# State-space projections in a new order, with two of five convolution taps on GpSimd

## The reference, cut to what matters

```python
zxbcdt = u @ w_in                                   # u: (256, 1024), w_in: (1024, 5184)
z   = zxbcdt[..., :2048]
xbc = silu(dwconv_centred(zxbcdt[..., 2048:5120], conv_w, conv_b))   # 5 taps, 3072 channels
dt  = softplus(zxbcdt[..., 5120:] + dt_bias)        # 64 step rows: 2 directions x 32 heads
x, B, C = xbc[:2048], xbc[2048:2560], xbc[2560:]    # B and C: 4 groups of 128 states
# context: only its final states are wanted:  sum over tokens of B^T (x * dt * decay), per group, both directions
# sequence: y = (C B^T * decay mask) (x dt) + C state * exp(cumulated decay), both directions, + d_skip x
# out = rmsnorm_by_group(y * silu(z)) @ w_out
```

## Time and profile before

| | us |
|---|---|
| median of three runs (lowest, highest) | 3063.94 (3062.34, 3069.13) |
| the profiled execution | 3061.89 |
| its span | 3060.1 |
| TensorE busy | 2890.5 |
| VectorE busy | 2267.7 |
| ScalarE busy | 1404.9 |
| GpSimd busy | 398.1 |

### The profile page before, as it was taken

One profiled execution on the slowest core, in us unless ns is written; L12 is line 12 of the kernel. 1 busy time (PEld: TensorE's weight loads), 2 busy tenths in 40 slices (PEclk: granted clock), 3 DMA queues, 4 the chain that ended last, 5 costly groups with the idle time before them and its releaser, 6 DMA issues.

```text
span 3060.1 us, 61776 instructions
## 1 busy us (share of the span) xinstructions
PE 2890.5 (94%) x24756; PEld 2772.1 (91%) x24756; DVE 2267.7 (74%) x3614; ACT 1404.9 (46%) x2279; POOL 398.1 (13%) x430
## 2 busy tenths in 40 slices
PE   5999999999999999999999999699989899999898
PEld 5999887899999988779999999599978899999898
DVE  7999565578878775556787888589867688777654
ACT  3446533444444563444444445544677344444342
POOL 0025001010200210200102012001026201102002
PEclk9999999999999999999999999799989899999899
DMA  9995302459968641125787885189522388676353
GB/s 342 350 373 158 124 9 97 131 191 326 335 232 283 214 152 64 54 72 186 255 319 263 312 324 170 58 309 327 186 82 72 132 302 322 235 261 212 111 186 131
DMA packets 172725, 632.19 MB, mean 207 GB/s; under 512 B 19169, under 2 KB 19553, under 8 KB 172001
## 3 DMA queue, kind: packets, MB, share of 16 engines
q1 hardware_dynamic: 123696, 450.79, 42.0%
q10 hardware_dynamic: 48816, 178.41, 16.9%
HBM read 628.07 MB, written 1.05 MB: 206 GB/s over the span
## 4 chain that ended last, share of the span: by engine, by line
PE 84%; DVE 11%; ACT 3%; issue 1%; DMA 1%; POOL 0%; DVEq 0%; ACTq 0%; POOLq 0%
PE psum L581 23%; PE psum L583 23%; PE psum L582 23%; DVE w_lo L549 3%; DVE xl L2151 2%; PE psum L599 1%; DVE ada_w L628 1%; PE psum L600 1%; DVE bc L2151 1%; PE psum L605 1%; PE psum L2299 1%; PE psum L1495 1%; PE psum L1498 1%; PE psum L2328 1%; PE psum L2219 1%
## 5 line engine op out<-in xcount | busy, mean ns | idle before, releaser
L581 PE MATMUL psum<-h_hi,w_hi 128*128 128x256 f32 x4464 | 1257.4, 282 | 1.2 <-ACT qn L1940 0.9
L582 PE MATMUL psum<-h_hi,w_lo 128*128 128x256 f32 x4464 | 1250.6, 280 | 0.0
L583 PE MATMUL psum<-h_lo,w_hi 128*128 128x256 f32 x4464 | 1249.0, 280 | 0.0
L549 DVE TENSOR_TENSOR w_lo<-raw,w_hi 128x1024 fp32r<-128x1024 f32 x852 | 1065.7, 1253 | 193.0 <-ACT w_hi L536 192.0
L536 ACT ACTIVATE w_hi<-raw 128x1024 fp32r<-128x1024 f32 x852 | 875.1, 1055 | 386.8 <-DMA raw<-stream_dram 229.4
L581 PEld LDWEIGHTS psum<-h_hi,w_hi 128*128 128x128 f32 x4464 | 843.1, 189 | 8.4 <-issue 5.3
L582 PEld LDWEIGHTS psum<-h_hi,w_lo 128*128 128x128 f32 x4464 | 843.3, 189 | 0.5
L583 PEld LDWEIGHTS psum<-h_lo,w_hi 128*128 128x128 f32 x4464 | 843.0, 189 | 0.0
L581 PE MATMUL psum<-u_hi,w_hi 128*128 128x256 f32 x1584 | 442.8, 280 | 0.0
L582 PE MATMUL psum<-u_hi,w_lo 128*128 128x256 f32 x1584 | 442.1, 279 | 0.0
L583 PE MATMUL psum<-u_lo,w_hi 128*128 128x256 f32 x1584 | 442.0, 279 | 0.0
(11 more groups left out here) (385 smaller groups left out, 3411.0 us busy)
## 6 DMA issues: line engine op xcount, KB each, us to landing
raw<-stream_dram SPq DMA_DIRECT2D x852, 512.0 KB, 4.2
ada_w<-ada_dram ACTq DMA_DIRECT2D x328, 512.0 KB, 4.7
tmp<-c_dram ACTq DMA_DIRECT2D x8, 512.0 KB, 3.7
x<-x_dram SPq DMA_DIRECT2D x1, 1024.0 KB, 9.9
ctx_x<-ctx_dram ACTq DMA_DIRECT2D x1, 1024.0 KB, 4.8
means<-means_dram ACTq DMA_DIRECT2D x1, 1024.0 KB, 4.8
out_dram<-tmp SPq DMA_DIRECT2D x1, 1024.0 KB, 3.9
const<-const_dram SPq DMA_DIRECT2D x1, 753.0 KB, 13.2
```

What stands on the lines that cost most here:

```text
L549: p.nc.vector.tensor_tensor(p.w_lo[:, slot].rearrange("p k m -> p (k m)"), p.raw[:, slot], p.w_hi[:, slot].rearrange("p k m -> p (k m)").b ...
L581: mm(out, p.w_hi[:, slot, k], hi, start=start, stop=False, skip_group_check=skip)
L582: mm(out, p.w_lo[:, slot, k], hi, start=False, stop=False, skip_group_check=skip)
L583: return mm(out, p.w_hi[:, slot, k], lo, start=False, stop=stop, skip_group_check=skip)
```

## The change

The units of the projections come as B, C, step rows, x (context: B, step rows, x). The separate state stage is gone. Between the units TensorE now turns finished pairs, makes the columns, B by C and, for the context, the states group by group (two behind units 15 and 19, two at the end); ScalarE copies them between its own steps and applies silu two tiles late instead of one. The step rows are computed right behind the first x tile. Weighted x (xw) is made per group and direction, 14 of the 16 instructions on GpSimd, two on VectorE. For the sequence GpSimd takes the middle tap with the bias (ScalarE's before) and tap 0 (VectorE's before), as two tensor_scalar and an add; VectorE keeps three taps. Z units 0 and 1 run between the last turned pairs, z unit t of the rest at step 2t-1 of the mixing loop (2t+1 before), and VectorE makes a gate behind the output in the same step, not before it. Some semaphores are shared under new names.

```diff
     dt = np.concatenate([w_in[:, 5120:5184], np.zeros((D, P - 64), np.float32)], 1)
-    return [by_tile(np.concatenate([xbc, dt], 1))]
+    xs, bc = xbc[:, : N_X * P], xbc[:, N_X * P :]
+    return [by_tile(np.concatenate([bc, dt, xs], 1))]
 
...
-        self.sconv_in = self.over("sconv_in", 32768, [P, 4, 264])
+        self.sconv_ctx = self.over("sconv_ctx", 32768, [P, 4, 264])
+        self.sconv_x = self.over("sconv_x", 65536, [P, 4, 264])
...
-        self.xw = self.over("xw", 0, [P, 2, 2048])
+        self.xw = self.over("xw", 65536, [P, 2, 2, 512])
+        self.tap = self.over("tap", 73728, [P, T])[:]
...
+SSD_BANKS = (5, 4, 7, 6)
+
+
+def turned_at(st, u):
+
+    if st.on_ctx and u in (6, 8):
+        return (u - 6) // 2
+    i = u - st.n_dt - 5
+    return 2 * st.on_ctx + i // 2 if i >= 0 and i % 2 == 0 and i // 2 < 6 else None
+
+
+def turned_pair(st, j):
+
+    if st.on_ctx:
+        return (N_X + 2 * j, N_X + 2 * j + 1) if j < 2 else (2 * j - 4, 2 * j - 3)
+    return 2 * j, 2 * j + 1
+
+
+def conv_tile(st, k):
+    return N_X + k if k < st.n_dt else k - st.n_dt
...
+    def turn(j):
+        s0, s1 = turned_pair(st, j)
+        pe.wait_ge(p.sem["act_done"], a("act_done") + (s1 - N_X + 1 if s1 >= N_X else s1 + n_bc + 1))
+        if j >= 2:
+            pe.wait_ge(p.sem["sturn_out"], a("sturn_out") + j - 1)
...
+        ins.then_inc(p.sem["sturned"], 1)
...
+    def columns_of(rows):
+        pe.wait_ge(p.sem["dt_ready"], a("dt_ready") + 1)
...
+        ins.then_inc(p.sem["cols_done"], 1)
+
+    def b_by_c(g):
+        pe.wait_ge(p.sem["act_done"], a("act_done") + N_BC + g + 1)
+        if g == 1:
+            pe.wait_ge(p.sem["cols_ready"], a("cols_ready") + 1)
+        if g >= 2:
+            pe.wait_ge(p.sem["cb_out"], a("cb_out") + g - 1)
...
+        ins.then_inc(p.sem["cb_done"], 1)
+
+    def state(g):
+        for d in range(2):
+            pe.wait_ge(p.sem["xw_ready"], a("xw_ready") + 2 * (2 * g + d) + 2)
+            if g:
+                pe.wait_ge(p.sem["state_out"], a("state_out") + 2 * g + d - 1)
...
+            ins.then_inc(p.sem["state_sum"], 1)
...
+    for u in range(2, st.n_conv + 1):
+        if u >= 4:
+            pe.wait_ge(p.sem["proj_out"], a("proj_out") + u - 3)
+        pe.wait_ge(p.sem["lo_ready"], u0 + u + 1)
         for k in range(UNIT):
...
+        if turned_at(st, u) is not None:
+            turn(turned_at(st, u))
+        if u == n_bc + 5:
+            columns_of(p.rows if st.on_ctx else p.soft)
+        if not st.on_ctx and u >= 12 and u % 2 == 0 and u < 20:
+            b_by_c((u - 12) // 2)
+        if st.on_ctx and u in (15, 19):
+            state((u - 15) // 4)
+    if st.on_ctx:
+        turn(last - 1)
+        turn(last)
+        state(2)
+        state(3)
+        pe.wait_ge(p.sem["state_out"], a("state_out") + 8)
     else:
-        for c in range(8):
-            one(1, c)
-    for c in range(st.n_conv % 8 + 1):
-        one(st.n_conv // 8, c)
+        pe.wait_ge(p.sem["proj_out"], a("proj_out") + st.n_conv - 1)
+        z_unit(p, pe, st.mix, 0)
+        turn(last - 1)
+        z_unit(p, pe, st.mix, 1)
+        turn(last)
 
 
 def ssd_in_scalar(p, act, st):
...
+    for u in range(st.n_conv + 1):
+        k = u if u < n_bc else u - 1
+        if u > 1:
+            split_hi(p, act, u0 + AHEAD + u)
+        act.wait_ge(p.sem["unit_done"], u0 + u + 1)
+        raw = p.psum[:, SSD_BANKS[u % 4], 0:T]
+        if u == n_bc:
+            f(p.rows[0:ROWS], raw[0:ROWS], ACT.Copy).then_inc(p.sem["proj_out"], 1)
+        else:
+            if k >= 4:
+                act.wait_ge(p.sem["conv_done"], a("conv_done") + k - 3)
+            t = conv_tile(st, k)
+            if st.on_ctx:
+                f(p.sxbc(t), raw, ACT.Identity, scale=w[:, t, 2:3], bias=bias[:, t : t + 1])
+            f(raw_in[:, k % 4, 2 : 2 + T], raw, ACT.Copy).then_inc(p.sem["proj_out"], 1)
+            if k >= 2:
+                silu(k - 2)
+        if u == n_bc + 1:
+            gate_steps(p, act, st)
+        if turned_at(st, u - 1) is not None:
+            turned(turned_at(st, u - 1))
+        if not st.on_ctx and u == n_bc + 3:
+            act.wait_ge(p.sem["dt_step"], a("dt_step") + 7)
+            f(p.row_parts[0:ROWS], p.rows[0:ROWS], ACT.Copy).then_inc(p.sem["gate_fn"], 1)
+        if not st.on_ctx and u > 12 and u % 2 and u < 21:
+            b_by_c((u - 13) // 2)
+        if st.on_ctx and u in (16, 20):
+            state((u - 16) // 4)
+    silu(st.n_conv - 2)
+    silu(st.n_conv - 1)
+    if turned_at(st, st.n_conv) is not None:
+        turned(turned_at(st, st.n_conv))
+    for j in range(2):
+        turned(6 + 2 * st.on_ctx + j)
+    if st.on_ctx:
+        state(2)
+        state(3)
...
 def ssd_in_gpsimd(p, pool, st):
...
+        norm_gpsimd(p, pool, st.next_norm)
+        pool.wait_ge(p.sem["cols_ready"], a("cols_ready") + 1)
+        for i in range(7):
+            weighted_x(p, pool, p.nc.gpsimd, st, i // 2, i % 2)
+        return
+    w = st.par(p, "conv").rearrange("p (t j) -> p t j", j=5)
+    bias, v = st.par(p, "conv_b"), p.nc.gpsimd
+    pool.wait_ge(p.sem["conv_pad"], a("conv_pad") + 8)
+    for k in range(st.n_conv):
+        u, t, src = k if k < st.n_dt else k + 1, conv_tile(st, k), raw_in[:, k % 4]
+        pool.wait_ge(p.sem["proj_out"], a("proj_out") + u + 1)
+        v.tensor_scalar(p.sxbc(t), src[:, 2 : 2 + T], w[:, t, 2:3], bias[:, t : t + 1], ALU.mult, ALU.add).then_inc(
+            p.sem["tap_step"], 1)
+        if k:
+            pool.wait_ge(p.sem["tap_done"], a("tap_done") + k)
+        v.tensor_scalar(p.tap, src[:, 0:T], w[:, t, 0:1], None, ALU.mult).then_inc(p.sem["tap_step"], 1)
+        pool.wait_ge(p.sem["tap_step"], a("tap_step") + 2 * k + 2)
+        v.tensor_tensor(p.sxbc(t), p.sxbc(t), p.tap, ALU.add).then_inc(p.sem["tap_done"], 1)
+
+
+def weighted_x(p, eng, engine, st, g, d):
+
+    a = st.at
+    eng.wait_ge(p.sem["sturn_out"], a("sturn_out") + 2 * g + 4)
+    if g:
+        eng.wait_ge(p.sem["state_sum"], a("state_sum") + 2 * g + d - 1)
+    heads, part = slice(d * SH + 8 * g, d * SH + 8 * g + 8), slice(g * 512, g * 512 + 512)
+    for c in range(2):
+        engine.tensor_tensor(
+            p.xw[:, d, c].rearrange("p (h n) -> p h n", h=8), p.x_tok[:, c, part].rearrange("p (h n) -> p h n", h=8),
+            p.scols[:, 0, c, heads].unsqueeze(2).broadcast_to([P, 8, 64]), ALU.mult,
+        ).then_inc(p.sem["xw_ready"], 1)
 
 
 def ssd_in_vector(p, dve, st):
-    a, u0, v = st.at, st.unit0, p.nc.vector
+    a, u0, v, n_bc = st.at, st.unit0, p.nc.vector, st.n_dt
     w = st.par(p, "conv").rearrange("p (t j) -> p t j", j=5)
-    dve.wait_ge(p.sem["conv_pad"], a("conv_pad") + 4)
-    for t in range(st.n_conv):
-        if t > 1:
-            split_lo(p, dve, u0 + AHEAD + t)
-        dve.wait_ge(p.sem["proj_out"], a("proj_out") + t + 1)
-        out, src = p.sxbc(t), p.sconv_in[:, t % 4]
-        for i, j in enumerate((0, 1, 3, 4)):
+    raw_in = p.sconv_of(st)
+    dve.wait_ge(p.sem["conv_pad"], a("conv_pad") + 8)
+    for k in range(st.n_conv):
+        u = k if k < n_bc else k + 1
+        if k == n_bc:
+            split_lo(p, dve, u0 + AHEAD + n_bc)
+        if u > 1:
+            split_lo(p, dve, u0 + AHEAD + u)
+        if st.on_ctx:
+            dve.wait_ge(p.sem["proj_out"], a("proj_out") + u + 1)
+        else:
+            dve.wait_ge(p.sem["tap_done"], a("tap_done") + k + 1)
+        t = conv_tile(st, k)
+        out, src, taps = p.sxbc(t), raw_in[:, k % 4], (0, 1, 3, 4) if st.on_ctx else (1, 3, 4)
+        for i, j in enumerate(taps):
             if i:
-                dve.wait_ge(p.sem["conv_step"], a("conv_step") + 3 * t + i)
+                dve.wait_ge(p.sem["conv_step"], a("conv_step") + (len(taps) - 1) * k + i)
             v.scalar_tensor_tensor(out, src[:, j : j + T], w[:, t, j : j + 1], out, ALU.mult, ALU.add).then_inc(
-                p.sem["conv_step" if i < 3 else "conv_done"], 1)
-    split_lo(p, dve, u0 + AHEAD + st.n_conv)
-    step = a("dt_step")
+                p.sem["conv_step" if i < len(taps) - 1 else "conv_done"], 1)
+        if k == n_bc:
+            step_rows(p, dve, st)
+        if k == n_bc + 3 and not st.on_ctx:
+            dve.wait_ge(p.sem["gate_fn"], a("gate_fn") + 6)
+            v.tensor_tensor(
+                p.row_parts[ROWS : 2 * ROWS], p.rows[0:ROWS], p.row_parts[0:ROWS].bitcast(F32), ALU.subtract
+            ).then_inc(p.sem["dt_ready"], 1)
+        if k == n_bc + 5:
+            dve.wait_ge(p.sem["cols_done"], a("cols_done") + 1)
+            v.tensor_copy(p.scols[:, 0].rearrange("p c r -> p (c r)"), p.psum[:, 3, 0 : 2 * ROWS]).then_inc(
+                p.sem["cols_ready"], 1)
+    if st.on_ctx:
+        dve.wait_ge(p.sem["cols_ready"], a("cols_ready") + 1)
+        dve.wait_ge(p.sem["xw_ready"], a("xw_ready") + 14)
+        weighted_x(p, dve, v, st, 3, 1)
...
         v.tensor_tensor(p.soft[0:ROWS], p.sin[0:ROWS], rows, ALU.subtract).then_inc(p.sem["dt_ready"], 1)
-
-
-
...
```

(38 more changed lines are left out.)

254 lines of the change are left out of this document (94 added, 160 removed).

## The result

The change makes the kernel slower: 3098.58 us (median of 5 runs, 3089.29 to 3103.80) beside 3069.13 for the kernel before on the same chip (5 runs, 3062.34 to 3073.48). The ratio is 1.0096, 95% interval 1.0077 to 1.0115, so +29.5 us. The forecast was 3077, that is +13 against its own reference of 3063.9; the sign is right, the size less than half of what came, and 3098.58 is above the range of 3060 to 3090.

What follows compares the result with a forecast made beforehand. TensorE, busy 94% of 3060.1 us, was taken as the bound. Context -17.7, sequence's projections +5.5 and mixing loop +24.9 gave +12.7, 3074.6 profiled, forecast 3077 at the median's offset; range 3060 to 3090.

Steps and rivals of the forecast that it cites:

- Part 1: Context projections up to the next norm's sum: 17.7 us saved, bounds -20 to -5.
- The price put on weighted x: Context: each 128x512 weighted x instruction on GpSimd taken at 1.25 us, between 0.9 and 3.4.
- Part 2: Sequence's projections up to the first exponential: 5.5 us longer, between -8 and +13.
- The columns' wait: Sequence's projections: TensorE stands 7.5 us behind unit 14, as VectorE copies the columns only after convolution 13.
- the one at turn 0: Sequence's projections: TensorE waits 5 us for silu 9 at turn 0, while the step rows hold ScalarE and GpSimd.
- that makes 2.9 us a tile: Sequence's convolutions: GpSimd's three new instructions, 0.53, 1.15 and 1.15 us, sum to 2.9 a tile, 3.5 at the upper end.
- rival 2: GpSimd bounds the sequence's convolutions at 3.5 to 3.8 us a tile, adding 6 to 10: 3085; chance 0.15.
- the tap saved is given back by the slower neighbours: Sequence's convolutions: VectorE's three taps and a split beside GpSimd take 3.14 us a tile, no less than four taps alone.
- Part 3: Mixing loop, first exponential to last products: 24.9 us longer than 112.2; +16.5 or +27 with other waits.
- The ring: Mixing loop's two z banks: z unit t needs the gate of t-2, so units 4 to 15 each wait 2.3 us.
- rival 1: The two z banks do not bind; the mixing loop is 2.7 us shorter: 3049; chance 0.12.
- A pair of steps takes 5.27 + 4.14: Mixing loop: 5.27 us until the z unit starts plus 4.14 for it and products, 9.4 instead of 7.07.

Runs made afterwards that it cites:

- e7_ctx_only: Kernel before with only the change's context part; sequence projections, turns and mixing loop stay old: 3046.96 us, ratio 0.9935 to the kernel before.
- e1_ring: Changed kernel with z units 2 to 15 put back from step 2t-1 to 2t+1: 3051.92 us, ratio 0.9967 to the kernel before.
- e2_gate_first: Changed kernel, z units still early, VectorE making the gate before the output: 3068.07 us, ratio 1.0013 to the kernel before.

## Why the prediction was right or wrong

**Part 1 was right.** Forecast -17.7 for the profiled execution, measured -16.3 in it and -17.8 in e7_ctx_only. The price put on weighted x, 1.25 us from no row, stands between what four took beside VectorE (5.52, 5.20, 4.81 us) and alone (2.04 for two):

```profile
1906.49 5.52 POOL L2286 TENSOR_TENSOR xw<-x_tok,scols 128x512 f32<-128x512 f32 x4 [31.93 <-ACT x_tok L2179]
...
1947.66 2.04 POOL L2286 TENSOR_TENSOR xw<-x_tok,scols 128x512 f32<-128x512 f32 x2 [5.37 <-PE psum L2127]
...
1907.46 4.82 DVE L2312 SCALAR_TENSOR_TENSOR xl<-sconv_ctx,par,xl 128x256 f32<-128x256 f32 x4
```

The third row is the disturbance: four taps of VectorE take 4.82 us beside it instead of 2.04, three times, 8 us in all where "some 5" were allowed. The step rows' wait was 4.4 where 5.8 follows from the forecast. Of the 6.7 at the turns of x, 5.5 is the wait ahead of the last turn, for which the forecast's tail has 0.9 + 2.0 + 0.8 = 3.7: the third disturbance falls on just these taps. The 1.2 at the turn ahead of it are near the 1.4 that the forecast gave to silu 5.

**Part 2 had the waits at the right places and GpSimd's part wrong.** The columns' wait (7.5 forecast, measured 7.2) and the one at turn 0 (5, measured 4.8) are there. They are only in part the order's own: with the early copy the first is 3.8, without GpSimd's taps they are 4.8 and 2.5, and with both edits 0.4 and 2.4. No run has GpSimd at the 2.9 us that the forecast worked with, so that its two waits came out nearly as measured, while GpSimd took more, is in part luck. The step that failed is "that makes 2.9 us a tile": 0.53, 1.15 and 1.15 became 0.79, 1.08 and 1.47, a tile each 3.40. That is rival 2's mechanism in part only: GpSimd is slower than VectorE and keeps it waiting, but it is not the bound of the stretch, since behind the columns TensorE's own work is. Of the 6 to 10 that rival 2 put on the forecast 3.2 came, though against four taps on VectorE the two taps cost 8.1. A second step failed with it: "the tap saved is given back by the slower neighbours". VectorE's taps and split went from 3.10 to 2.8 a tile, and it then waited for GpSimd. From 243 to 270 us VectorE was indeed slowed by its neighbour; in the sequence's projections the neighbour hardly slowed it, it kept it waiting. A slip in the same sum: from 244.33 to 268.48 there are 22 starts and so 21 gaps, 1.15 us each and not 1.10, and 1.21 without the two short ones; with it a tile is still under 3.0 and nothing in the forecast changes.

The rule of the Trainium skill, GPSIMD Engine Reference, Key points, on instructions of two SBUF inputs, agrees here: VectorE's four taps took 4.82 beside weighted x, and GpSimd's add took 1.47 beside VectorE's split, which reads two, where it had taken 0.74 beside none. The one-input rate of the same page's Engine selection, against which the forecast argued, would give 0.5 for the product, as an estimate; it took 1.08.

**Part 3 had the right mechanism, and its sum lacked a term.** The ring binds, at units 4 to 15, twelve times, for a gate that stands behind the output: rival 1 falls, e1_ring and e2_gate_first show it. The wait was put at 2.3 and is 1.81 (the z unit starts 4.9 us after the even rows, not 5.2, and would be there after 3.1, not 2.93). The step that failed is "A pair of steps takes 5.27 + 4.14 (z unit and products, ...) = 9.4" (5.23 by its own terms, 0.5 us in all): the 4.14 behind the wait were taken at the full clock, though the same text, in part 2, charged clock for pauses by the 0.77 of the earlier trace rows. A pair takes 10.67. In the terms of the sum: waits 21.8 us instead of 27.6, lower clock 14 to 17 instead of 0, less the 2.7 of the two units that left the loop. With that term the upper bound of part 3 would have been some 42 (an estimate, 27 and 14 to 17) and the range would have held the result.

**The sum** then: -16.3 + 1.0 + 8.7 + 36.5 = +29.9 in the profile, +29.5 between the medians. The expectation that the loop "can be spoilt" was the right lead, and most of the chance, 0.71, stood rightly on slower.

## What to carry to other kernels

Where a loop keeps TensorE full, a unit moved one step earlier in a ring of two must be checked against the chain that frees its bank: a pause of 1.8 us per turn of the loop cost nearly twice its length, because the clock fell behind it. If the pause can't be removed, shorten it by the order on the releasing engine, or fill it: eight spare matmuls in each pause made this kernel some 12 us faster. As placed here they spoilt its values, so a place for what they write has to be found first. Before work is handed to GpSimd, add up its instructions per tile and compare with the tile's time, and then ask what latency it puts between two engines: a helper that is fast enough on the mean still delays each point where the order waits.
